# Merge gates as a token-major Strassen product ahead of everything, in a differential-attention and latent-attention encoder block

## The reference

```python
h = _rmsnorm(x, norm_g[layer])
proj = h @ w_in[layer]                     # 2048 x 10304
aq, ak, av, ag, cq, ckv, kr, bg, mg = jnp.split(proj, SPLIT_POINTS, axis=-1)
oa = _diff_attention(...)                  # 8 heads, two softmaxes each, ALiBi
ya = (oa.reshape(b, s, A_WIDTH) * jax.nn.silu(ag)) @ w_oa[layer]
ob = _mla_attention(q_nope, q_rope, k_nope, k_rope, vb)   # 8 heads
yb = (ob.reshape(b, s, B_WIDTH) * jax.nn.silu(bg)) @ w_ob[layer]
ga, gb = jnp.split(mg, 2, axis=-1)         # the merge gates, 512 x 4096
merged = jax.nn.sigmoid(ga) * ya + jax.nn.sigmoid(gb) * yb
x = x + merged @ w_out[layer]
return _rmsnorm(x, final_g)
```

## Time and profile before

| what | value |
| --- | --- |
| median of three runs | 1507.8 us |
| profiled execution, its own time | 1507.93 us |
| its span, first to last instruction | 1506.1 us |
| TensorE busy | 1485.6 us, 6996 matmuls recorded |
| VectorE, ScalarE, GpSimd busy | 765.5, 518.5, 35.1 us |
| moved by DMA | 140.46 MB, mean 93 GB/s |
| granted clock, mean | 0.999 |

### The profile page before, as it was taken

The page is one execution under the profiler, slowest core; times in us unless marked ns, Lnnn a source line. Parts: engine busy times, 40 slices in busy tenths (PEclk is TensorE's granted clock), DMA queues, the critical chain, the costliest instruction groups (busy, mean ns, idle before and its releaser), DMA issues.

```text
span 1506.1 us, 19432 instructions
## 1 busy us (share of the span) xinstructions
PE 1485.6 (99%) x6996; PEld 1242.0 (82%) x6996; DVE 765.5 (51%) x1157; ACT 518.5 (34%) x781; POOL 35.1 (2%) x58
## 2 busy tenths in 40 slices
PE   6999999999999999999999999999999999999997
PEld 5888888888888888888888888888888888888886
DVE  6667566666656547777778232222223222253431
ACT  6333434434433334434445222222222222242321
POOL 0000000000000000000000000000000000000000
PEclk9999999999999999999999999999999999999999
DMA  6322222222222332222222333333333333344422
...
DMA packets 236277, 140.46 MB, mean 93 GB/s; under 512 B 18640, under 2 KB 223568, under 8 KB 235728
## 3 DMA queue, kind: packets, MB, share of 16 engines
...
...
## 4 chain that ended last, share of the span: by engine, by line
PE 97%; issue 1%; DMA 1%; DVE 0%; ACT 0%; SPq 0%; POOLq 0%; POOL 0%; DVEq 0%; ACTq 0%
PE bank L1241 30%; PE bank L1243 30%; PE bank L1242 30%; PE bank L1296 2%; PE bank L1270 1%; PE bank L1273 1%; DMA w_raw<-in_w_in_dram 1%; PE bank L1327 1%; PE bank L1321 1%; PE bank L1292 0%; PE bank L1288 0%; PE bank L1289 0%; PE bank L1291 0%; PE bank L1287 0%; PE bank L1350 0%
## 5 line engine op out<-in xcount | busy, mean ns | idle before, releaser
L770 DVE TENSOR_TENSOR w_lo<-w_raw,w_hi 128x1024 fp32r<-128x1024 f32 (+1 forms) x238 | 288.3, 1211 | 534.8 <-ACT w_hi L451 533.9
L1241 PE MATMUL bank<-h_hi,w_hi 128*128 128x512 f32 x1296 | 509.6, 393 | 0.5 <-DVE k_hl L775 0.3
L1243 PE MATMUL bank<-h_hi,w_lo 128*128 128x512 f32 x1296 | 504.9, 390 | 0.0
L1242 PE MATMUL bank<-h_lo,w_hi 128*128 128x512 f32 x1296 | 504.7, 389 | 0.0
L451 ACT ACTIVATE w_hi<-w_raw 128x1024 fp32r<-128x1024 f32 (+1 forms) x238 | 249.9, 1050 | 569.3 <-DMA w_raw<-in_w_in_dram 340.1
L1243 PEld LDWEIGHTS bank<-h_hi,w_lo 128*128 128x128 f32 x1296 | 243.3, 188 | 51.5
L1241 PEld LDWEIGHTS bank<-h_hi,w_hi 128*128 128x128 f32 x1296 | 243.5, 188 | 49.9 <-DVE k_hl L775 0.7
L1242 PEld LDWEIGHTS bank<-h_lo,w_hi 128*128 128x128 f32 x1296 | 243.6, 188 | 48.3
L471 ACT ACTIVATE e<-e,small 128x512 f32<-128x512 f32 x64 | 45.8, 716 | 139.5 <-DVE small L801 139.5
L1241 PE MATMUL bank<-w_hi,mg_hi 128*128 128x512 f32 x224 | 87.1, 389 | 0.0
L1242 PE MATMUL bank<-w_lo,mg_hi 128*128 128x512 f32 x224 | 87.1, 389 | 0.0
...
## 6 DMA issues: line engine op xcount, KB each, us to landing
...
```

The costliest lines, as they stand in the source:

```text
L770: dve.tensor_tensor(w_lo[:, piece.slot, 0:cols], w_raw[:, piece.slot, 0:cols], w_hi[:, piece.slot, 0:cols].bitcast(F32), ALU.subtract).the ...
L1241: pe.matmul(dst, lhs_hi, rhs_hi, start=start, stop=False)
L1242: pe.matmul(dst, lhs_hi, rhs_lo, start=False, stop=False)
L1243: return pe.matmul(dst, lhs_lo, rhs_hi, start=False, stop=stop)
```

## The change

The merge gates are computed first, before the heads, token-major, with Strassen's scheme (Winograd's form, 7 products for 8). Tokens and features are halved: A11 and A12 are the features' halves for tokens 0 to 255, A21 and A22 for tokens 256 to 511. The 4096 gate columns make four groups of 1024, each halved to 512. A block product is 256 tokens x 1024 features x 512 columns. The sums of blocks of h are made once: S1 = A21 + A22, S2 = S1 - A11, S3 = A11 - A21, S4 = A12 - S2 (S1 on VectorE, the others on GpSimd), each then split in hi and lo. The sums of weight blocks are made for each row of features as it comes.

The stage has 72 steps (`MergeStep`), one per piece of raw weights, in a ring of four slots of 8 KB per partition (`m_raw`; `m_lo` overwrites it) and three of `m_hi`:

- P, steps 0 to 7 of group 0: A11 and then A12 by weight blocks alone, two feature tiles per step, 12 matmuls.
- A0, steps 8 to 15 of group 0: products with S2, S1 and A22, three weight sums, 18 matmuls.
- B0, steps 16 to 23 of group 0: products with S3 and S4, one weight sum, 12 matmuls.
- X, eight steps for each of groups 1 to 3 (24 to 31, 40 to 47, 56 to 63): products with A11, S1, S2, A22 (four), three weight sums, 1 MB of weights, 24 matmuls.
- Y, eight steps each (32 to 39, 48 to 55, 64 to 71): products with A12, S3, S4 (three), one weight sum, 768 KB of weights, 18 matmuls.

The weights of a group are so read almost twice. VectorE adds the products from PSUM (`sum_...`), ScalarE takes the sigmoids and sends them to DRAM (`gates`, 8 MB) with DMAs of its own. x is loaded tile by tile with the weights of the first pieces between; the tokens of x tiles 2 and 3 are turned while P runs. A second split of h for tokens 256 to 511 ("late") lies in steps 8 to 10 (the rest of a first one) and 33 to 36. The heads come after. The merge at the end becomes `Y_UNITS`: 8 units of 512 columns, one branch each, token-major, 4 steps of 24 matmuls; the gates are read back from DRAM, VectorE multiplies and adds (`gate_y`, `add_y`), TensorE turns `merged` (64 transposes of 128 x 128 that were not there), and ScalarE and VectorE split it from PSUM. `ga_hi` and `ga_lo` are made in quarters.

```diff
+        self.raw, self.hi = n % M_RAW, n % M_HI
+        self.landed = 32 * (n // M_RAW + 1)
+        if n < 8:
+            self.kind, self.g, self.k = "P", 0, 2 * (n % 4)
+        elif n < 24:
+            self.kind, self.g, self.k = ("A0", "B0")[n >= 16], 0, n % 8
+        else:
+            self.kind, self.g, self.k = ("X", "Y")[(n - 24) % 16 >= 8], 1 + (n - 24) // 16, n % 8
+        self.first = self.k == 0
+        self.final = self.k == (6 if self.kind == "P" else 7)
+        p0, p1 = {"P": (0, 2), "A0": (1, 4), "B0": (0, 2), "X": (0, 4), "Y": (0, 3)}[self.kind]
+        self.cols = slice(p0 * SEQ, p1 * SEQ)
...
+            def merge_piece(n):
+                st = MERGE[n]
+                if n >= M_RAW:
+                    sp.wait_ge(m_used, n - (M_RAW - 1))
+                raw = m_raw[:, st.raw, :]
+                col = MG + st.g * GROUP
...
+                    parts = [(raw[:, 0:2 * SEQ], block(top, 0, GROUP)), (raw[:, 2 * SEQ:4 * SEQ], block(low, 0, GROUP))]
+                elif st.kind == "B0":
...
+                    parts = [(raw[:, 0:SEQ], block(top, SEQ, SEQ)), (raw[:, SEQ:3 * SEQ], block(low, 0, GROUP))]
+                for dst, src in parts:
+                    sp.dma_start(dst, src).then_inc(m_in[st.raw], 16)
...
+            def y_piece(i):
+                cb, branch = Y_UNITS[i // U_STEPS]
+                w = (w_oa, w_ob)[branch]
+                piece = Piece(Y0 + i)
+                raw = w_raw[:, piece.slot, :].rearrange("p (k c) -> p k c", k=2)
+                load(piece, [(raw[:, j:j + 1, :], rows(w, 2 * (i % U_STEPS) + j, 1, cb * SEQ, SEQ)) for j in range(2)])
...
+            def full_a(m):
+                pool.wait_ge(h_lo_ready, m + 1)
+                k = 2 * m
+                dst = s34_raw[:, k % HALF_K:k % HALF_K + 2, k // HALF_K, :]
+                pool.tensor_tensor(dst, h_hi[:, k:k + 2, 0:HALF_T].bitcast(F32), h_lo[:, k:k + 2, 0:HALF_T].bitcast(F32),
+                                   ALU.add).then_inc(f_ready, 1)
+            def combine(j):
+                ks = slice(2 * j, 2 * j + 2)
+                s1, s2 = s12_raw[:, ks, 0, :], s12_raw[:, ks, 1, :]
+                s3, s4 = s34_raw[:, ks, 0, :], s34_raw[:, ks, 1, :]
+                pool.wait_ge(s1_ready, j + 1)
+                if j == 0:
+                    pool.wait_ge(f_ready, KT // 2)
+                pool.tensor_tensor(s2, s1, s3, ALU.subtract).then_inc(s2_ready, 1)
+                pool.wait_ge(s2_ready, j + 1)
+                pool.tensor_tensor(s4, s4, s2, ALU.subtract).then_inc(s4_ready, 1)
+                pool.tensor_tensor(s3, s3, h_raw[:, ks, HALF_T:SEQ], ALU.subtract).then_inc(s3_ready, 1)
...
+            def merge_hi(n):
+                st = MERGE[n]
+                if st.kind == "P":
+                    act.wait_ge(m_in[st.raw], st.landed)
+                else:
+                    act.wait_ge(m_sum, n - 7)
+                if n >= M_HI:
+                    act.wait_ge(m_used, n - (M_HI - 1))
+                act.activation(m_hi[:, st.hi, st.cols], m_raw[:, st.raw, st.cols], ACT.Copy).then_inc(m_hi_ready, 1)
...
+            def keep_p2(g):
+                if g < M_GROUPS - 1:
+                    act.wait_ge(m_used, 24 + 16 * g)
+                else:
+                    act.wait_ge(a_full, M_GROUPS)
+                if g > 1:
+                    act.wait_ge(c11_ready, g)
+                act.activation(post_z[:, :], DUO_A[:, :], ACT.Copy).then_inc(p2_ready, 1)
...
+                act.wait_ge(c11_ready, g + 1)
+                act.activation(buf[:, :], buf[:, :], ACT.Sigmoid).then_inc(g11_ready, 1)
+                act.wait_ge(g11_ready, g + 1)
...
+            def merge_step(n):
+                if n < N_MERGE and MERGE[n].kind == "X" and MERGE[n].final:
+                    keep_p1(MERGE[n].g)
+                if n + AHEAD < N_MERGE:
+                    merge_hi(n + AHEAD)
+                if n < N_MERGE and MERGE[n].kind == "Y" and MERGE[n].final:
+                    keep_p2(MERGE[n].g)
+                if n == 9:
+                    gate11(0)
+                if 8 <= n < 11:
+                    late_hi(n - 7)
+                if 10 <= n < 14:
...
+                    end = 23 + 16 * g
+                    if n == end + 1:
+                        gate22(g)
...
+            def merge_lo(n):
+                st = MERGE[n]
+                dve.wait_ge(m_hi_ready, n + 1)
+                dve.tensor_tensor(m_lo[:, st.raw, st.cols], m_raw[:, st.raw, st.cols],
+                                  m_hi[:, st.hi, st.cols].bitcast(F32), ALU.subtract).then_inc(m_lo_ready, 1)
...
+            def merge_sums(n):
+                st = MERGE[n]
+                p = [m_raw[:, st.raw, i * SEQ:(i + 1) * SEQ] for i in range(4)]
+                def first(dst, a, b, n_first=1):
+                    firsts[0] += 1
+                    dve.tensor_tensor(dst, a, b, ALU.subtract).then_inc(m_first, 1)
+                dve.wait_ge(m_in[st.raw], st.landed)
+                if st.kind == "Y":
+                    dve.tensor_tensor(p[0], p[2], p[0], ALU.subtract).then_inc(m_sum, 1)
+                elif st.kind in ("A0", "X"):
+                    first(p[1], p[1], p[0])
+                    dve.wait_ge(m_first, firsts[0])
+                    seconds[0] += 1
+                    dve.tensor_tensor(p[3], p[3], p[1], ALU.subtract).then_inc(m_second, 1)
+                    dve.wait_ge(m_second, seconds[0])
+                    dve.tensor_tensor(p[2], p[3], p[2], ALU.subtract).then_inc(m_sum, 1)
+                else:
+                    dve.tensor_tensor(p[0], p[1], p[0], ALU.subtract).then_inc(m_sum, 1)
...
+            def sum_u3_c22(g):
+                dve.wait_ge(b_full, 2 * g + 2)
+                dve.wait_ge(w_ready, g + 1)
+                dve.tensor_tensor(post_u2[:, :], DUO_B[:, :], post_u2[:, :], ALU.add).then_inc(u3_ready, 1)
+                if g:
+                    dve.wait_ge(g22_out, 16 * g)
+                else:
+                    dve.wait_ge(g11_out, 16)
+                dve.tensor_tensor(post_x[:, :], DUO_B[:, :], post_w[:, :], ALU.add).then_inc(c22_ready, 1)
...
+            def merge_step(n):
+                if n + 1 < N_MERGE:
+                    merge_lo(n + 1)
+                for g in range(M_GROUPS - 1):
+                    if n == 23 + 16 * g:
+                        sum_u3_c22(g)
+                        sum_c21(g)
+                        sum_c12(g)
+                if n + AHEAD < N_MERGE:
+                    merge_sums(n + AHEAD)
+                if n == 8:
+                    sum_c11(0)
+                if 8 <= n < 11:
+                    late_lo(n - 7)
+                if 11 <= n < 15:
+                    s34_lo_of(n - 11)
+                if 33 <= n < 37:
+                    late_lo(n - 29)
+                for g in range(M_GROUPS):
+                    end = 23 + 16 * g
...
-            def branch_b(i, b):
-                n = i * 2 + (b + 1)
-                dve.wait_ge(used, i * M_STEPS + (M0 + 6 * b + 6))
-                dve.wait_ge(sig_ready, i * 4 + (2 * b + 2))
-                dve.tensor_tensor(part[:, 1, :], bank[4 * b + 3][:, :], sig[:, b, 1, :], ALU.mult).then_inc(part_b, 1)
-                dve.wait_ge(part_a, n)
-                dve.wait_ge(part_b, n)
-                dve.tensor_tensor(merged[:, bass.ds(i * (2 * SEQ) + b * SEQ, SEQ)], part[:, 0, :], part[:, 1, :],
-                                  ALU.add).then_inc(merged_ready, 1)
...
+            def gate_y(u, t):
+                cb, branch = Y_UNITS[u]
+                if t < TOK - 1:
+                    dve.wait_ge(y_done, (TOK - 1) * u + t + 1)
+                else:
+                    dve.wait_ge(used, Y0 + U_STEPS * (u + 1))
+                if t == 0:
+                    dve.wait_ge(sig_in[u % 2], 16 * (u // 2 + 1))
+                    if branch == 0 and cb >= 2:
+                        dve.wait_ge(m_turned, 4 * (cb - 1))
+                    if branch and cb:
+                        dve.wait_ge(merged_ready, TOK * cb)
+                dst = merged[:, cb % 2, t, :] if branch == 0 else part[:, t, :]
+                dve.tensor_tensor(dst, y_bank(u, t)[:, :], sig[:, u % 2, t, :], ALU.mult).then_inc(y_read, 1)
...
+            def product(st, dst, which, part_no, start, stop, k=None):
+                c = slice(part_no * SEQ, (part_no + 1) * SEQ)
+                for j in range(2):
+                    hi, lo = block_of(which, st.k if k is None else k, j)
+                    last = three(dst[:, j * SEQ:(j + 1) * SEQ], hi, lo, m_hi[:, st.hi, c], m_lo[:, st.raw, c],
+                                 start, stop)
+                return last
...
+                    if st.first:
+                        p6()
+                        p4()
+                        p5()
+                        last = p1()
...
+            def y_block(u, i, t, halves):
+                branch = Y_UNITS[u][1]
+                g_hi, g_lo = (ga_hi, ga_lo) if branch == 0 else (gb_hl[:, :, 0, :], gb_hl[:, :, 1, :])
```

(17 more changed lines are left out.)

901 lines of the change are left out of this document (674 added, 227 removed).

## The result

The changed kernel takes 1558.0 us (median of 4 runs, 1557.0 to 1558.3) where the kernel before took 1507.8. The ratio is 1.0331, 95% interval [1.0314, 1.0349]: 3.3% slower. The forecast was 1545 us with a range of 1522 to 1568. The sign and the range held; the forecast lay 13 us too low (+37 us where +50 came).

A forecast was written before the change was run, and what follows sets the result against it. TensorE, 99% busy, bounds the kernel before; afterwards gate weight preparation makes it wait. -43.5 - 3.8 + 68.2 + 7.2 + 1 = +29, plus 6 (GpSimd) and 2 (clock), gives +37 on 1507.9: 1545 us, range 1522 to 1568.

The forecast's parts named there:

- What goes: Gate stage: 1344 matmuls instead of 1536, 192 fewer at 0.2267 us each, 43.5 us saved.
- the start: Before the first product: ScalarE squares two x tiles instead of four, first matmul at 15.8 us, -3.8 us.
- The ring: Gate weight preparation: sums, copy and subtraction run one after another, 6.3 us per X step against 5.44 of matmuls.
- Rival B: Gate stage: the ring is no bound because pieces can run ahead, 1473 us; chance 4%.
- P and A0: Group 0, steps 0 to 15: TensorE waits 5 us in P and 18.7 us in A0.
- GpSimd: Early gate stage: GpSimd's 20 two-input sums and VectorE's work may exclude each other, 6 us (bounds 0 and 14).
- Rival A: Early gate stage: GpSimd and VectorE exclude each other fully, 14 us instead of 6, 1553 us; chance 33%.
- The last head: Last head's steps: TensorE waits for a quarter of ga_lo and VectorE's reading of Y tiles, 1 us (0 to 6).
- the transposes: Behind the gate stage: 64 uncovered transposes of merged at 0.11 us each, 7.2 us.
- The clock: Gate stage: TensorE comes back slowly from idle stretches, mostly hidden, 2 us (bounds 0 and 10).
- rival C: Gate stage: the clock falls in the waits and stays low, X steps 10.9 us, near 1600 us; chance 7%.
- Transfers at 0: DMA of weight pieces and gates: priced at 0, with 6 us if P's pieces come late.

The follow-up runs named there:

- h1: The changed kernel with a fourth linked 512-column sum in each X piece: 1575.7 us.
- f1: The changed kernel with A0 and X pieces copied and subtracted in two parts, the first part's copy starting behind the first sum: 1529.9 us.
- e2: The changed kernel with GpSimd writing zeros in place of its twenty two-input sums: 1544.9 us.
- e4: The changed kernel with the copy and subtraction of output piece Y0+4 put behind the step's other copies in the last head: 1550.7 us.
- e1: The changed kernel with VectorE making the sums of piece n+2 before it subtracts piece n+1: 1537.0 us.
- g4: The changed kernel with halved copies, reordered group changes, the later output piece, GpSimd's sums on VectorE, and S3/S4 and C11 work moved to later steps: 1508.2 us.
- e3: The changed kernel with each of the 64 transposes of merged made twice: 1564.6 us.

## Why the forecast was right, and where 13 us were missing

1. **What goes, and the start.** What goes held: TensorE has 132 instructions fewer (6996 to 6864: 192 matmuls less, 64 transposes more, 4 warm-up matmuls less), and the pitch is 0.2267 us as before. The start did not: -3.8 us were taken, bounds -6 and 0, and +0.1 came. I had counted ScalarE's squares and not what stands on TensorE, sixteen warm-up matmuls ahead of the second tile's transposes.
2. **The ring.** Its intervals held to 0.1 us in X, Y, A0 and B0 steps and at the group change. h1 shows that it bounds in the X steps, f1 that it is the linked order sums, copy, subtraction that makes it.
3. **Rival B** (pieces can run ahead, 1473) fell for the reason given: the order of instructions. In f1 its condition is met for the X steps, and the kernel takes 1529.9 us all the same, not 1473: B also left out the waits at the start and at the group changes.
4. **P and A0.** From the `m_lo` of step 8 to that of step 15 44.3 us were forecast. e2, in which GpSimd doesn't disturb, has 44.0; the changed kernel 46.1. The `m_lo` of step 15 ends at 95.5 us in e2, against 15.8 + 26.2 + 5 + 3 + 44.3 = 94.3 forecast. That this is so close is in part luck: e2's first product begins at 19.2 us, 3.4 late, and P then takes 2 us less than forecast.
5. **GpSimd: the step that failed.** I took 6 us from bounds of 0 and 14. e2 measured 13.1 and moved the `m_lo` of step 15 by 13.7. Rival A was the right case; its price of 14 us, from 45 us of work in 31, was good to 1 us, or to 4 if GpSimd's order is taken off. The argument against it (VectorE would have to want the port at every moment) was wrong: VectorE had an operation in hand or waiting for its turn during 14.93 of 15 us. The Trainium skill ("SBUF — State Buffer", "SBUF: two separate sides") says the two lock each other out of the shared port pair; the trace agrees in kind, with 1.22 us drawn out to 2.28. A rule that is on the page and a trace that is silent should have been given more than a third of the chance.
6. **The last head: the second term too small.** 1 us taken, bounds 0 and 6; e4 measured 7.3, outside the bounds (5.4 of wait, the rest the clock behind it). I had looked at VectorE's load and not at what stands behind a wait for a reused buffer in ScalarE's order.
7. **The sum.** 6.3 us from the last head and 7.1 from GpSimd make 13.4, the size of the gap of 13 us, but they don't make it up alone. Step by step, TensorE's starts give: start +3.9 against the forecast; P and A0 +3.8 (13 us from GpSimd where 8 were set for it and the clock, 1.4 less for the rest); B0, group changes, X and Y -2.1; the last head +6.3; the transposes -0.6; 1.9 left open. Two misses, the missing start and waits that were put too high, nearly cancel. The first head's matmuls follow the stage at 406.7 us, outside the 395 to 405 that were given.
8. **The clock** was put at 2 us, and rival C (near 1600) did not come: the mean was 0.99. It fell in single places, behind waits of 5.4 to 5.7 us (step 8, the first group change, the last head); behind 3.46 us (at 86.67) the next matmul took 0.50 us and those after it 0.40, full speed. TensorE in the changed kernel, step 8:

```profile
63.17 0.79 PE L1758 MATMUL duo<-m_hi,s_hi 128*128 128x512 f32 x1 [5.56 <-DVE m_lo L1218]
63.76 0.63 PE L1759 MATMUL duo<-m_lo,s_hi 128*128 128x512 f32 x1
64.19 0.63 PE L1760 MATMUL duo<-m_hi,s_lo 128*128 128x512 f32 x1
...
67.60 0.48 PE L1759 MATMUL duo<-m_lo,s_hi 128*128 128x512 f32 x1
67.92 0.40 PE L1760 MATMUL duo<-m_hi,s_lo 128*128 128x512 f32 x1
```

   Nine matmuls follow each other at 0.43 us, twice the pitch of 0.23 (1.2 instead of 2.4 GHz): 2 us more. In step 8 the wait for the next `m_lo` covers it; in the last head nothing does. X steps, which idle 0.59 us each, ran at full clock. The swinging of the Trainium skill's page ("TensorE: Matmul & The Clock Gate", "HAM oscillation — how this bites in real kernels") did not come in them; the page's own case has a wait of several us in every tile, so these steps don't speak against it.
9. **Transfers at 0** held in the changed kernel. In e1, where the order asked for pieces sooner, VectorE waited 64 us for them, of which TensorE felt little (2.9 us at the end of B0). In f1 VectorE waited 7.5 us and in g4 19.0; whether that cost time was not tested.
10. **The transposes** were forecast at 7.2 us; e3 measured 6.6.
